# Attention with the values as the stationary operand of two heads at a time, and the probabilities scaled on GpSimd

## The reference, cut to what matters

```python
s = einsum('bqhd,bkhd->bhqk', qn, k_nope) + einsum('bqhr,bkr->bhqk', qp, k_pe)
p = softmax(s * scale, axis=-1)
o = einsum('bhqk,bkhd->bqhd', p, v)          # 12 heads of 64 columns
out = concatenate([f, o], axis=-1) @ w_out   # f: Fourier part, 256 columns
```

## Time and profile before

| | |
|---|---|
| median of 3 executions | 908.78 us (908.47 to 909.54) |
| span of the profiled execution | 906.0 us, first to last instruction |
| its own time | not listed apart; the three executions lie 2.5 to 3.5 us above the span |
| PE busy | 817.3 us (90%) |
| DVE, ACT, POOL busy | 258.3, 155.2, 65.8 us |
| attention heads on PE | from 555.7 us (first scores) to 627.5 us (last output transpose) |

### The profile page before, as it was taken

The page is one execution under the profiler, slowest core; times in us unless marked ns, Lnnn a source line. Parts: engine busy times, 40 slices in busy tenths (PEclk is TensorE's granted clock), DMA queues, the critical chain, the costliest instruction groups (busy, mean ns, idle before and its releaser), DMA issues.

```text
span 906.0 us, 10566 instructions
## 1 busy us (share of the span) xinstructions
PE 817.3 (90%) x4129; PEld 463.2 (51%) x4130; DVE 258.3 (29%) x569; ACT 155.2 (17%) x324; POOL 65.8 (7%) x102
## 2 busy tenths in 40 slices
PE   3899999999989999999669998999998999999970
PEld 0446665443865555555344553676446645545530
DVE  0201211112341221221450432454145121221226
ACT  2100000101321111111031111543022111112101
POOL 2000000000000000000321000000000000000005
PEclk9899999999679999999879998999996999999995
DMA  9987243949908999636690526412022392579514
GB/s 339 314 246 286 93 162 122 365 149 382 399 1 319 396 396 378 275 112 237 233 380 0 192 93 247 172 34 107 0 107 103 143 405 101 242 289 359 238 62 177
DMA packets 64141, 195.99 MB, mean 216 GB/s; under 512 B 11456, under 2 KB 18624, under 8 KB 51056
## 3 DMA queue, kind: packets, MB, share of 16 engines
q1 hardware_dynamic: 57216, 179.09, 52.0%
q10 hardware_dynamic: 4016, 10.20, 3.0%
q0 software_dynamic: 2880, 6.30, 1.8%
HBM read 187.56 MB, written 12.21 MB: 220 GB/s over the span
## 4 chain that ended last, share of the span: by engine, by line
PE 84%; DVE 5%; DMA 5%; issue 2%; POOL 1%; SPq 1%; ACT 1%; ACTq 0%; POOLq 0%; DVEq 0%
PE ps L1126 16%; PE ps L1106 14%; PE ps L1145 8%; PE ps L1192 7%; PE ps L1053 7%; PE ps L1010 5%; DMA pool<-in_mod_w 4%; PE ps L1246 4%; PE ps L1179 3%; PE ps L1356 2%; PE ps L1208 2%; PE ps L1328 2%; PE ps L1291 2%; PE ps L1061 2%; PE ps L1028 2%
## 5 line engine op out<-in xcount | busy, mean ns | idle before, releaser
L1126 PE MATMUL ps<-pool 128*64 128x512 f32 x640 | 141.7, 595 | 5.9 <-issue 5.9
L1106 PEld LDWEIGHTS ps<-pool,xn 128*128 128x128 f32 x1056 | 124.5, 194 | 39.4 <-issue 39.4
L1106 PE MATMUL ps<-pool,xn 128*128 128x128 f32 x1056 | 133.9, 281 | 4.2 <-DVE pool L702 4.2
L1126 PEld LDWEIGHTS ps<-pool 128*64 128x64 f32 x640 | 45.4, 137 | 88.0 <-issue 87.5
L1053 PE MATMUL ps<-pool,yT 128*128 128x512 f32 x192 | 83.0, 593 | 0.0
L1145 PE MATMUL ps<-pool 128*64 128x512 f32 x320 | 73.1, 598 | 0.0
L1010 PE MATMUL ps<-pool,cs 128*32 128x512 f32 x384 | 53.7, 623 | 17.4 <-ACT cs L537 8.4
L1192 PE MATMUL ps<-hT,pool 128*128 128x384 f32 x192 | 62.1, 486 | 0.0
L1053 PEld LDWEIGHTS ps<-pool,yT 128*128 128x128 f32 x192 | 36.4, 190 | 45.5 <-issue 45.4
L796 DVE COPY pool<-ps 128x1024 f32<-128x1024 f32 x20 | 24.5, 1225 | 115.5 <-PE ps L1145 115.5
L1192 PEld LDWEIGHTS ps<-hT,pool 128*128 128x128 f32 x192 | 37.7, 196 | 24.5 <-issue 0.5
(11 more groups left out here) (192 smaller groups left out, 823.1 us busy)
## 6 DMA issues: line engine op xcount, KB each, us to landing
pool<-in_moe_w SPq DMA_DIRECT2D x96, 1024.0 KB, 9.2
pool<-in_mod_w SPq DMA_DIRECT2D x20, 2048.0 KB, 14.3
pool<-in_mod_w SPq DMA_DIRECT2D x8, 1024.0 KB, 14.8
pool<-in_ev_w_in SPq DMA_DIRECT2D x6, 1024.0 KB, 10.4
pool<-in_ev_w_in SPq DMA_DIRECT2D x2, 2048.0 KB, 11.3
pool<-in_ev_w_out SPq DMA_DIRECT2D x2, 2048.0 KB, 11.6
pool<-in_od_w_out SPq DMA_DIRECT2D x2, 2048.0 KB, 10.3
pool<-in_od_w_in SPq DMA_DIRECT2D x2, 1856.0 KB, 9.1
```

Source lines behind the costliest of these rows:

```text
L1106: ins = mm(bank2(2, D)[:, cc * P:(cc + 1) * P], xn[:, t, cc * P:(cc + 1) * P], select[:, t, :], start=t == 0, stop=t == TILES - 1)
L1126: ins = mm(ps[m, 0, :], hTe.rearrange("p (c n) -> p c n", c=DC)[:, cc, m], w13[e][:, :, cc, :], start=cc == 0, stop=cc == DC - 1)
```

## The change

Per pair of heads, the values become the stationary operand (128 keys x 64 columns) and the turned probabilities move: 128 columns for query tile 0, and 256 for tiles 1 and 2 together, cut from `prT` with a stride. The even head's output goes to partitions 0 to 63 of bank 1, the odd head's to 64 to 127, alternating. The output is then already turned, so one copy for a pair puts it into `yT`, and `o`, its 18 transposes and their three copies go. A turned output cannot be scaled by a number per partition, so the probabilities are scaled before they are turned: DVE takes the reciprocal and counts up `pinv`, POOL multiplies the three pieces of the head by it and counts up `probs_even`, and PE's transposes wait for that. `pr_s`, `prT` and `pinv` get a second buffer. PE does the values of a pair in the even iteration two heads later. ACT and DVE move their copies of the turned probabilities.

```diff
+            for h in range(NH):
+                gps.wait_ge(S("pinv"), h + 1)
+                for t in range(TILES):
+                    ins = nc.gpsimd.tensor_scalar(probs(h, t), probs(h, t), pinv[:, h % 2, t:t + 1], None, ALU.mult)
+                ins.then_inc(S("probs_even"), 1)
...
+            def probs_out(h):
+
+                act.wait_ge(S("p_tr"), h + 1)
+                if h >= 2:
+                    act.wait_ge(S("o_mm"), h // 2)
+                a_.activation(prT[h % 2][:, 0:512], ps[:, 4, :], ACT.Copy).then_inc(S("pT_act"), 1)
+
             k_pair(0)
+            act.wait_ge(S("new_kv"), 32)
             for h in range(NH):
...
                 ins.then_inc(S("probs"), 1)
                 if h % 2 == 0 and h + 2 < NH:
                     k_pair(h // 2 + 1)
-                act.wait_ge(S("p_tr"), h + 1)
-                a_.activation(prT[:, 0:512], ps[:, 4, :], ACT.Copy).then_inc(S("pT_act"), 1)
+                if h:
+                    probs_out(h - 1)
+            probs_out(NH - 1)
...
             for h in range(NH):
+                head_sums(h)
                 if h + 1 < NH:
                     head_maxima(h + 1)
                 if h % 2 and h + 2 < NH:
                     head_q(h + 2)
-                if h:
-                    head_out(h - 1)
+                if h and h % 2 == 0:
+                    pair_out(h // 2 - 1)
                 if h % 2 == 0 and h + 2 < NH:
                     head_q(h + 2)
-                head_probs_out(h)
...
+                probs_out(h)
+            pair_out(NH // 2 - 1)
...
-                pe.wait_ge(S("probs"), h + 1)
+                pe.wait_ge(S("probs_even"), h + 1)
+                if h:
+                    pe.wait_ge(S("pT_act"), h)
+                    pe.wait_ge(S("pT_dve"), h)
...
+            def pair_values(g):
+
+                pe.wait_ge(S("pT_act"), 2 * g + 2)
+                pe.wait_ge(S("pT_dve"), 2 * g + 2)
+                if g:
+                    pe.wait_ge(S("o_out"), g)
+                for kt in range(4):
+                    for b in range(2):
+                        h, m = 2 * g + b, slice(b * VD, (b + 1) * VD)
+                        if kt == 0:
+                            ins = mm(ps[m, 1, 0:P], vv[:, 0, h * VD:(h + 1) * VD], prT[b][:, 0:P], start=True, stop=True)
+                        else:
+                            keys = prT[b][:, P:7 * P].rearrange("p (t k n) -> p t k n", t=2, k=3)[:, :, kt - 1, :]
+                            ins = mm(ps[m, 1, P:T].rearrange("p (t n) -> p t n", t=2), vv[:, kt, h * VD:(h + 1) * VD], keys,
+                                     start=kt == 1, stop=kt == 3)
                 ins.then_inc(S("o_mm"), 1)
...
-                if h:
-                    head_values(h - 1)
+                if h and h % 2 == 0:
+                    pair_values(h // 2 - 1)
                 if h % 2 == 0 and h + 2 < NH:
                     head_q(h + 2)
                 head_probs(h)
-            head_values(NH - 1)
-            pe.wait_ge(S("o_out"), NH)
-            for t in range(TILES):
-                for k in range(6):
-                    ins = tr(bank2(2 * t, 6 * P)[:, k * P:(k + 1) * P], o[:, t, k * P:(k + 1) * P], ident)
-                ins.then_inc(S("o_tr"), 1)
+            pair_values(NH // 2 - 1)
+            pe.wait_ge(S("o_out"), NH // 2)
```

More of the change, by code:

```diff
@@ L122, in program @@
         z = scratch(3456, 3 * Z_END, OB).rearrange("p (t n) -> p t n", t=3)
-        o = scratch(3456, 3 * NH * VD, OB).rearrange("p (t n) -> p t n", t=3)
         qT = scratch(6240, 2 * T, OB).rearrange("p (b n) -> p b n", b=2)
         kT = scratch(7008, 1024, OB).rearrange("p (b n) -> p b n", b=2)
-        pr_s = scratch(8032, 896, OB)
-        prT = scratch(8928, 896, OB)
+        pr_s = [scratch(at, 7 * P, OB) for at in (8032, 3456)]
+        prT = [scratch(at, 7 * P, OB) for at in (8928, 4352)]
         rtmp = scratch(8032, 768, OB).rearrange("p (k n) -> p k n", k=4)
@@ L133, in program @@
         psum_of = scratch(9830, 6, OB).rearrange("p (b t) -> p b t", b=2)
-        pinv = scratch(9836, 3, OB)
+        pinv = scratch(9836, 6, OB).rearrange("p (b t) -> p b t", b=2)
         ktmp = scratch(9840, 64, OB).rearrange("p (k n) -> p k n", k=4)
@@ L157, in scores, with probs @@
             return (ps[:, b, 0:P], ps[:, b, P:512], ps[:, b + 1, 0:T])[t]
-        def probs(t):
-            return pr_s[:, (0, P, P + T)[t]:(P, P + T, P + 2 * T)[t]]
+        def probs(h, t):
+            return pr_s[h % 2][:, (0, P, P + T)[t]:(P, P + T, P + 2 * T)[t]]
         R, at = {}, 0
@@ L582, in k_pair @@
                 ins.then_inc(S("kT"), 1)
+            def probs_out(h):
[3 more added lines that the diff above has]
+                a_.activation(prT[h % 2][:, 0:512], ps[:, 4, :], ACT.Copy).then_inc(S("pT_act"), 1)
             k_pair(0)
+            act.wait_ge(S("new_kv"), 32)
             for h in range(NH):
                 act.wait_ge(S("nmax"), h + 1)
+                if h >= 2:
+                    act.wait_ge(S("p_tr"), h - 1)
                 for t in range(TILES):
-                    ins = a_.activation(probs(t), scores(h, t), ACT.Exp, bias=nmax[:, h % 2, t:t + 1], scale=SCALE,
+                    ins = a_.activation(probs(h, t), scores(h, t), ACT.Exp, bias=nmax[:, h % 2, t:t + 1], scale=SCALE,
                                         accum_out=psum_of[:, h % 2, t:t + 1])
@@ L929, in _, with head_sums, probs_out, pair_out @@
                 v_.tensor_copy(vv[:, kt, :], bank2((6, 3)[kt % 2], NH * VD)).then_inc(S("vv"), 1)
-            def head_probs_out(h):
+            def head_sums(h):
                 dve.wait_ge(S("probs"), h + 1)
-                if h:
-                    dve.wait_ge(S("o_out"), h)
-                v_.reciprocal(pinv, psum_of[:, h % 2])
+                if h >= 2:
+                    dve.wait_ge(S("probs_even"), h - 1)
+                v_.reciprocal(pinv[:, h % 2], psum_of[:, h % 2]).then_inc(S("pinv"), 1)
+            def probs_out(h):
                 dve.wait_ge(S("p_tr"), h + 1)
[L938 to L943, removed]
+                if h >= 2:
+                    dve.wait_ge(S("o_mm"), h // 2)
+                v_.tensor_copy(prT[h % 2][:, 512:7 * P], ps[:, 5, 0:7 * P - 512]).then_inc(S("pT_dve"), 1)
+            def pair_out(g):
+                dve.wait_ge(S("o_mm"), g + 1)
+                v_.tensor_copy(yT[:, 2 + g, :], ps[:, 1, 0:T]).then_inc(S("o_out"), 1)
             dve.wait_ge(S("new_kv"), 32)
@@ L1312, in head_probs @@
             def head_probs(h):
-                pe.wait_ge(S("probs"), h + 1)
+                pe.wait_ge(S("probs_even"), h + 1)
+                if h:
+                    pe.wait_ge(S("pT_act"), h)
+                    pe.wait_ge(S("pT_dve"), h)
                 for m in range(7):
-                    ins = tr(bank2(4, 7 * P)[:, m * P:(m + 1) * P], pr_s[:, m * P:(m + 1) * P], ident)
+                    ins = tr(bank2(4, 7 * P)[:, m * P:(m + 1) * P], pr_s[h % 2][:, m * P:(m + 1) * P], ident)
                 ins.then_inc(S("p_tr"), 1)
[L1319 to L1329, removed]
+            def pair_values(g):
[12 more added lines that the diff above has]
+                                     start=kt == 1, stop=kt == 3)
                 ins.then_inc(S("o_mm"), 1)
@@ L1380, in _ @@
                 head_probs(h)
-            head_values(NH - 1)
-            pe.wait_ge(S("o_out"), NH)
-            for t in range(TILES):
-                for k in range(6):
-                    ins = tr(bank2(2 * t, 6 * P)[:, k * P:(k + 1) * P], o[:, t, k * P:(k + 1) * P], ident)
-                ins.then_inc(S("o_tr"), 1)
+            pair_values(NH // 2 - 1)
+            pe.wait_ge(S("o_out"), NH // 2)
             pe.wait_ge(*L(4, "mod_col", 1))
             gate_rows(1, 0)
-            pe.wait_ge(S("y_att"), 3)
             arrived(pe, "out1.0")
```

4 lines of the change are left out of this document (removed).

## The result

The change takes 924.56 us (median of 4 executions, 923.79 to 924.71), the kernel before beside it 909.08 (908.47 to 909.54, 4 executions): a ratio of 1.017, 95% interval 1.0144 to 1.0196. The forecast was 916.2 with a range up to 924.5. The direction holds; the loss is 15.5 us where 7.4 were forecast, and the time lies just outside the range.

The account below looks back on a forecast made before the run. The prediction took PE's own order of work and the waits in it as the bound. 908.8 plus 4 x 2.27 - 5 x 0.35 - 1.6 + 1.7 = +7.4 gave 916.2 us, range 912.5 to 920, widened to 924.5.

Parts of the forecast that it names:

- ACT's order: Four even iterations: PE's values wait 1.89 us for ACT's probability copy behind two key copies; +2.27 us per iteration in all.
- 1.64 + 0.25: A pair's values on PE: 1.64 us with column halves overlapping, plus 0.25 for restarting after a wait.
- the first rival: Column halves do not overlap in the values: 3.00 us for 1.64, six times, +8.2, 924.4 us; chance 0.08.
- faster* rival: ACT's copy behind the key pair is ready in time, so even iterations' waits go: 905.9 us; chance 0.05.
- DVE's chain in odd iterations: Next scores wait for DVE's maxima, negation and query copy, taking most of the gain: -0.35 us per odd iteration.
- I take 1.5, nearer the memset: POOL's scaling of 896 columns was priced at 1.5 us a head, between 0.8 and 2.7.
- upper bound of 2.7: Highest price for POOL's scaling, us a head, from a two-input addition at 3.0 ns a column.
- 2.0 us a head: Odd iterations: POOL's scaling stays hidden behind the query path up to this time, so costs nothing at 1.5.
- the tail: From last scores to gate rows: 12.13 us becomes 10.5, -1.6, with POOL exposed only before head 11's transposes.
- The third rival: POOL becomes the wait at 2.7 us a head, in five odd iterations and the tail: +4.7, 920.9 us; chance 0.10.
- the second rival: The clock falls at most of the waits: four more low stretches, +6.8, 923.0 us; chance 0.13.
- one low stretch, 1.7 us: PE's new waits were charged one stretch at the 1.2 GHz clock, +1.7 us; five (+8.5) was the other end.

Follow-up runs that it names:

- e1: The changed kernel with ACT's copy of the turned probabilities put ahead of its two key copies; 918.1 us, ratio to before 1.0098.
- e3: The changed kernel without POOL's scaling and with ACT's copy of turned probabilities ahead of the key copies; 905.2 us, ratio to before 0.9959.
- e2: The changed kernel without POOL's scaling, outputs not divided by the row sums; 910.8 us, ratio to before 1.003.
- e6: The changed kernel with the scaling on DVE instead of POOL and ACT's copy ahead of the key copies; 908.1 us, ratio to before 0.9989.
- e4: The changed kernel with dummy matmuls on PE ahead of its two kinds of waits, results unread; 919.7 us, ratio to before 1.0106.
- e7: The changed kernel with scaling on DVE, ACT's copy ahead of key copies, DVE's query copy ahead of the maxima; 902.3 us, ratio to before 0.9933.
- e11: The kernel of e7 run once more, unchanged, for a second profile; 901.8 us, ratio to before 0.9925.
- e5: The changed kernel with POOL multiplying by the constant 0.125 instead of the reciprocal of the row sum; 924.0 us, one execution.
- e8: The changed kernel with POOL scaling only two of a head's three query tiles; 917.2 us, ratio to before 1.0092.
- e10: The changed kernel with ACT's copy ahead of key copies and DVE's query copy ahead of the maxima, scaling on POOL; 916.0 us, ratio 1.0089.

## Why the prediction was right and wrong

**ACT's order: right.** The wait of 1.89 before the values of even iterations is 1.92, four times: 7.7 of the row's 8.4; the rest is the last pair's 0.7. ACT starts the key copies when the pair is done and PE starts 0.04 after the third copy. The values took 0.44 + 1.30 = 1.74 for 1.64 + 0.25. So the halves overlap, and the first rival falls: not overlapped they would have been 3.00. The *faster* rival falls too, but its place was right: e1 takes this wait away.

**DVE's chain in odd iterations: right, and covered up.** The forecast wait for the query copy is there as soon as POOL is out of the way (e3, 0.97). Two heads in e2, 12.29, are near what the prediction had for its own assumption of a hidden POOL: 10.52 + 2.27 - 0.35 = 12.44.

**The term that failed: "I take 1.5, nearer the memset".** POOL takes 3.04 us a head, twice that, and above the upper bound of 2.7. The cover, "2.0 us a head", was nearly right: 2.2. Past it, two steps of the sum turn:
- odd iterations: +0.83 each where nothing was charged. At full clock two heads cost 2.60 more, not 1.92: 0.68 x 4 = 2.7 us over the four pairs shown.
- the tail: "head 11 waits for ... the whole of POOL (0.98 + 1.5 = 2.48)". The wait is 3.87, and head 10, charged with none, waits 0.69. With the last odd iteration that is 0.83 + 1.39 + 0.69 = 2.9.

The bound itself was badly made. 3.03 us for an addition of 1024 columns is one instruction; I took 3.0 ns a column for 896 and left out that three instructions have three starts. Built from the slope and start that the runs show, 3 x 0.28 + 896 x 2.5 ns = 3.08. And the choice between the ends was wrong by its reason: a memset reads nothing. The nearest row was the addition, since the price on POOL hardly depends on one input or two: 0.28 + 1024 x 2.5 ns = 2.84 for it, against 3.03 measured. The third rival had this mechanism, and its place, with 2.7 as the price and 0.10 as the chance.

The Trainium skill (GPSIMD Engine Reference, Engine selection) calls one-input elementwise work on GpSimd roughly line-rate. The runs contradict that for this shape: 2.5 ns a column against DVE's 0.5. Its advice in the same row, elementwise work on VectorE, is what e6 shows to be right.

**The clock: the second rival came true in part.** I took one low stretch, 1.7 us. In the trace the low clock costs +0.7 at the first heads (10.2 us of it instead of 6.8), 1.66 in the pair from 592.63, 2.2 from the last turning to the values, 2.2 at the gate rows: 6.8, hence +5.1. (Of the gate rows' 2.2, 0.3 is their start behind a wait: at full clock in e4 they take 3.80 for 3.53.) But not at "most of the waits": of four pairs with much the same waits, 1.92 + 1.80 us, one ran low, behind its wait of 1.80 for POOL. The big place is behind the wait of 3.87, which is POOL's again. In e4's trace 4.7 us of it are gone.

The other traces tie this term to POOL, but not its size. No run without POOL's scaling (e2, e3, e6, e7, e11) has a low stretch between the first heads and the gate rows, and of the six that have it only e4, with the dummy matmuls, has none. All the others fall to the low level in the tail, but for different lengths: some 10 us in the change and in e5, 7 in e1, 3 in e8 and e10, although e1 and e10 have the same wait of 3.87 as the change. In e1 and e10 the gate rows ran at full clock, 3.79 us. So how much of the 5 us an execution pays differs from one to the next.

**The account.** POOL 2.7 + 2.9, clock 5.1, the part ahead of the heads -2.5, behind the gate rows +1.0: 9.2, where the span is 16.8 - 7.4 = 9.4 above the forecast. The last two are not explained by the change; the code there is the same, and the part ahead moved by up to 7.5 us between profiles. That the sum closes to 0.2 us holds for this pair of profiles alone.

What stays open: why the clock falls behind one wait of 1.8 and not behind the next, why it stays low for 10 us behind one wait of 3.87 and for 3 behind another, and why the medians of e6 and e7 are 5.9 us apart where their attentions are 0.4 apart. e7's two heads are 0.95 shorter, but its first heads ran 10.2 us at the low level and e6's 3.4 (16.19 us up to the first turning for 13.59), which hides that gain in these two profiles; more of them would be needed.

## What to carry to other kernels

Before an elementwise step goes to GpSimd, find its price a column and a start for each instruction in a row that also reads and writes (here 2.5 ns and 0.28 us, where VectorE had 0.5 ns and 0.22 us), and compare it with the cover of each iteration, the last ones above all, where the cover is gone. When a change takes work out of an engine's list, ask what that work covered: here three waits came up, each in the order of another engine's list, and only with all three dealt with did the saved matmuls show. Compare the changed part between two points that both programs have, since code ahead of it can differ by several microseconds from one execution to the next.

## What the runs showed of the hardware

- GpSimd's scaling is this slow by itself, not by contention. At 631.76 in the tail DVE has nothing to do until 636.56, and the three instructions take 3.04 there as everywhere.
- VectorE's short scaling of three columns (L974), usually 0.17 us, took 0.36 at 587.94, 0.24 us after the start of POOL's third instruction (588.94 - 1.24 = 587.70):

```profile
583.30 0.17 DVE L974 TENSOR_SCALAR pool<-pool 128x3 f32<-128x3 f32 x1
...
585.90 3.04 POOL L444 TENSOR_SCALAR pool<-pool 128x128 f32<-128x128 f32 x3 [1.81 <-DVE pool L951]
...
587.94 0.36 DVE L974 TENSOR_SCALAR pool<-pool 128x3 f32<-128x3 f32 x1
```

The overlap alone is not enough. At 583.30 the same instruction falls into POOL's third one as well, which runs from 582.84 to 584.08, but 0.46 us behind its start, and takes the usual 0.17. Both end 0.6 us behind the start of POOL's instruction. Why is not shown.

The Trainium skill (SBUF — State Buffer, SBUF: two separate sides) describes the port pair which the two share as an exclusive lock between a GpSimd instruction and a VectorE one that runs in a two-port mode or reads two tensors from SBUF, with the loser blocked for the whole instruction. The row at 587.94 agrees that GpSimd can delay VectorE; a wait until 588.94 it does not show, and no run here tells the mode of L974.
